# Two scatter-adds under way inside one expert, and the mark that frees an output slot moved behind GpSimd's split

## What is computed

```python
def block_fn(args):
    tok, w, e = args
    return swiglu(x_pad[tok], we_gate[e], we_up[e], we_down[e]) * w[:, None]

ys = lax.map(block_fn, (row_tok.reshape(n_blocks, MOE_BLOCK), row_w.reshape(n_blocks, MOE_BLOCK), block_e))
out = jnp.zeros((n_tok + 1, d), hf.dtype).at[row_tok].add(ys.reshape(n_rows, d))
```

## Time and profile before

| | us |
|---|---|
| median of 3 runs | 2760.79 (2759.81 to 2764.53) |
| the profiled execution's span | 2760.2 |
| TensorE busy in it | 2543.3 (92%) |
| GpSimd busy | 1397.6 (51%) |
| VectorE / ScalarE busy | 1569.3 / 1141.9 |

### The profile page before, as it was taken

The page is one execution under the profiler, slowest core; times in us unless marked ns, Lnnn a source line. Parts: engine busy times, 40 slices in busy tenths (PEclk is TensorE's granted clock), DMA queues, the critical chain, the costliest instruction groups (busy, mean ns, idle before and its releaser), DMA issues.

```text
span 2760.2 us, 49351 instructions
## 1 busy us (share of the span) xinstructions
PE 2543.3 (92%) x11232; PEld 1855.3 (67%) x11233; DVE 1569.3 (57%) x2796; ACT 1141.9 (41%) x1514; POOL 1397.6 (51%) x1726
## 2 busy tenths in 40 slices
PE   5999999998899997999999999999999999999980
PEld 2754665534466666777787877788877777787770
DVE  4689969986676775333343344435544554454535
ACT  5133222233233232344444444445555555555532
POOL 2011123024666664455555555566777677766751
PEclk9999999997899999999999999999999999999995
DMA  8262604465232325677777777788988898888978
GB/s 249 96 126 73 214 27 66 170 239 175 100 107 93 107 77 207 167 198 198 196 193 205 202 194 219 205 252 234 286 258 257 262 292 258 258 257 260 268 213 293
DMA packets 304953, 534.61 MB, mean 194 GB/s; under 512 B 38597, under 2 KB 204485, under 8 KB 304120
## 3 DMA queue, kind: packets, MB, share of 16 engines
q1 hardware_dynamic: 250248, 352.77, 38.7%
q0 software_dynamic: 51472, 173.70, 26.4%
q10 hardware_dynamic: 3168, 7.34, 0.7%
HBM read 395.75 MB, written 138.00 MB: 193 GB/s over the span
## 4 chain that ended last, share of the span: by engine, by line
PE 37%; issue 17%; POOL 9%; POOLq 7%; DVE 2%; DMA 1%; ACT 0%; SPq 0%; another core or an unknown queue 0%; ACTq 0%
PE psm L1168 27%; PE psm L1112 6%; POOL arena L2366 3%; PE psm L1161 2%; POOL arena L2363 2%; POOL st L2356 2%; POOLq L2362 2%; POOLq L2384 1%; POOLq L2383 1%; POOLq L2375 1%; POOL arena L2376 1%; PE psm L1190 1%; PE psm L1136 1%; POOL acc_d L2380 1%; POOL st L2388 1%
## 5 line engine op out<-in xcount | busy, mean ns | idle before, releaser
L1168 PE MATMUL psm<-whi,xhi 128*128 (+1 forms) x1424 | 574.3, 403 | 37.5 <-issue 24.6
L1168 PE MATMUL psm<-whi,xlo 128*128 (+1 forms) x1424 | 557.9, 392 | 0.0
L1168 PE MATMUL psm<-wlo,xhi 128*128 (+1 forms) x1424 | 556.9, 391 | 0.0
L2097 DVE TENSOR_TENSOR arena<-psm,arena 128x256 f32<-128x256 f32 x178 | 75.5, 424 | 603.3 <-ACT arena L1574 603.3
L1168 PEld LDWEIGHTS psm<-whi,xhi 128*128 128x128 f32 x1424 | 268.6, 189 | 109.6 <-issue 58.5
L2371 POOL TENSOR_TENSOR wlo<-raw,whi (+1 forms) x64 | 330.8, 5169 | 18.6 <-ACT whi L1606 18.6
L1168 PE MATMUL psm<-whi,hhi 128*128 (+1 forms) x712 | 295.5, 415 | 21.9 <-POOL wlo L2371 14.6
L1574 ACT ACTIVATE arena<-psm 128x256 f32<-128x256 f32 x178 | 68.5, 385 | 578.7 <-PE psm L1168 573.7
L2380 POOL DMA_INDIRECT acc_d<-arena x162 | 278.9, 1722 | 56.2 <-issue 51.1
L1168 PEld LDWEIGHTS psm<-whi,xlo 128*128 128x128 f32 x1424 | 268.2, 188 | 57.7
L1168 PEld LDWEIGHTS psm<-wlo,xhi 128*128 128x128 f32 x1424 | 269.1, 189 | 51.0
(11 more groups left out here) (387 smaller groups left out, 3996.3 us busy)
## 6 DMA issues: line engine op xcount, KB each, us to landing
raw<-in_we_gate_dram SPq DMA_DIRECT2D x64, 1024.0 KB
raw<-in_we_up_dram SPq DMA_DIRECT2D x64, 1024.0 KB
raw<-in_we_down_dram SPq DMA_DIRECT2D x64, 1024.0 KB, 5.1
arena<-in_w_ada_dram SPq DMA_DIRECT2D x12, 2048.0 KB
arena<-in_x_dram SPq DMA_DIRECT2D x32, 512.0 KB, 4.2
h_d<-arena SPq DMA_DIRECT2D x17, 512.0 KB, 2.7
arena<-in_w_in_dram SPq DMA_DIRECT2D x16, 512.0 KB, 5.4
mix_d<-bo SPq DMA_DIRECT2D x32, 256.0 KB, 2.3
```

Source lines behind the costliest of these rows:

```text
L1168: m = TE.matmul(o, a, w, start=(n == 0), stop=(n == len(todo) - 1))
L2097: tt(htmp, psm[:, bank, 0:DE], sigb, ALU.mult).then_inc(s_hm_ready, 1)
```

## The change

Scatter n no longer waits for the landing of scatter n - 1, unless its block begins an expert. To tell landings apart there are two semaphores, one for each slot (`s_ya_out0`, `s_ya_out1`), and two index columns. VectorE makes a row `fences` once, in `block_rows`: for each block the count that the *other* slot's semaphore must have reached before its scatter goes. It is 16 times the number of earlier blocks in that slot, one fewer of them where the block does not begin an expert, and at least 16; so inside an expert the wait asks only for the scatter three back. GpSimd fills the row `turns` from which it is made with an `iota` ahead of the routed stage. In the step, the wait for the scatter of block b - 2 and its mark now come last, behind the scatter and the split. Behind the loop, the last scatter still waits for its predecessor.

```diff
@@ block_rows (VectorE)
+                dve.wait_ge(s_turns_ready, 1)
+                do(V.tensor_copy(rone[:, 0:NB], turns))
+                do(stt(rone[:, 0:NB], news[:, 1:NB + 1], 16.0, rone[:, 0:NB], ALU.mult, ALU.add))
+                do(ts(fences, rone[:, 0:NB], 16.0, None, ALU.max))
                 V.tensor_copy(splits, bef).then_inc(s_br_ready, 1)
@@ GpSimd, before the table is read back
+            for o in (s_bo_out0, s_bo_out1):
+                pool.wait_ge(o, 16 * (len(bok) // 2))
+            PO.iota(turns, pattern=[[16, NB // 2], [0, 2]], base=0, channel_multiplier=0).then_inc(s_turns_ready, 1)
@@ add_block
-            def add_block(b, w):
+            def add_block(b, w, first=False):
                 c = pool.value_load(berow[0:1, bass.ds(b + (3 * P - NT), 1)], min_val=0, max_val=NCOL - 2)
-                PO.tensor_copy(idxs, tabl[:, bass.ds(c, 1), 0].bitcast(U32)).then_inc(s_idy_ready, 1)
+                PO.tensor_copy(idxs[w], tabl[:, bass.ds(c, 1), 0].bitcast(U32)).then_inc(s_idy_ready, 1)
+                if not first:
+                    x = pool.value_load(fences[0:1, bass.ds(b - (NT + 1), 1)], min_val=16, max_val=16 * NB)
+                    pool.wait_ge([s_ya_out0, s_ya_out1][1 - w], x)
                 pool.wait_ge(s_idy_ready, b - (NT - 1))
                 pool.wait_ge(s_y_act, b + 1)
                 hold()
-                PO.indirect_dma_start(acc_d, bass.IndirectOffsetOnAxis(idxs, 0), yb[w], None, compute_op=ALU.add).then_inc(s_ya_out, 16)
+                PO.indirect_dma_start(acc_d, bass.IndirectOffsetOnAxis(idxs[w], 0), yb[w], None, compute_op=ALU.add)\
+                  .then_inc([s_ya_out0, s_ya_out1][w], 16)
@@ step
                 gather(b + 3, b - (NT - 4), 1 - w)
-                if not first:
-                    pool.wait_ge(s_ya_out, (b - (NT + 1)) * 16)
-                    PO.tensor_tensor(st[:, 59:60], mhalf[:, :], mhalf[:, :], ALU.add).then_inc(s_y_free, 1)
-                add_block(b - 1, 1 - w)
+                add_block(b - 1, 1 - w, first)
                 with pool.If(f > 0):
                     split_low((o & 1) * WSLOT, o + 1)
+                if not first:
+                    pool.wait_ge([s_ya_out0, s_ya_out1][w], ((b - (NT + 2)) >> 1) * 16 + 16)
+                    PO.tensor_tensor(st[:, 54 + w:55 + w], mhalf[:, :], mhalf[:, :], ALU.add).then_inc(s_y_free, 1)
@@ behind the loop
-            before = pool.value_load(nbm[0:1, 0:1], min_val=TOPK - 1, max_val=NB)
-            pool.wait_ge(s_ya_out, before * 16)
+            pool.wait_ge(s_ya_out0, nb * 8)
             PO.tensor_tensor(st[:, 59:60], mhalf[:, :], mhalf[:, :], ALU.add).then_inc(s_y_free, 1)
-            add_block(nb + (NT - 1), 1)
-            pool.wait_ge(s_ya_out, nb * 16)
+            add_block(nb + (NT - 1), 1, first=True)
+            pool.wait_ge(s_ya_out1, nb * 8)
```

More of the change, by code:

```diff
@@ L363, in build @@
         s_idy_ready = sem("idy_ready")
-        s_ya_out = sem("ya_out")
+        s_ya_out0 = sem("ya_out0")
+        s_ya_out1 = sem("ya_out1")
+        s_turns_ready = sem("turns_ready")
         UNITS = [(g, k) for g in range(2) for k in range(KD)]
@@ L532, in build @@
         nbm = cut2(1, dt=I32, base=W)
-        idxs = cut2(1, dt=U32, base=W)
+        idxs = [cut2(1, dt=U32, base=W) for _ in range(2)]
         bef, news, rone = (cut2(NROW, base=W)[0:1, :] for _ in range(3))
@@ L545, in build @@
         ordi, splits = (ytok[0:1, n * NROW:(n + 1) * NROW].bitcast(I32) for n in range(2))
+        turns, fences = (bof[0:1, 5 * P + n * (NROW - 2):5 * P + (n + 1) * (NROW - 2)].bitcast(I32) for n in range(2))
         xg = [xbr[:, 0:1024], xbr[:, 1024:2048]]
```

## The result

The changed kernel takes 2723.6 us (median of 4 runs, 2719.33 to 2727.93) where the kernel before took 2762.66 beside it (4 runs, 2759.81 to 2766.76): a ratio of 0.9861, 95% interval 0.9837 to 0.9885. The forecast was 2724. The profiled execution spans 2717.6 us against 2760.2.

What follows compares the result with a forecast made beforehand. TensorE, nearly always busy in the routed stage, was taken as the bound, with gains only from its idle time there and from the end. Terms summed to 36.6 us less than 2760.79: forecast 2724 us, 8-in-10 range 2704 to 2764.

Steps and rivals of the forecast that it cites:

- 1, the wait for GpSimd's split: Before `down`: TensorE's wait for GpSimd's split goes, as scatters inside an expert no longer wait; -14.6 us.
- 3, the large stall: Where GpSimd's split meets VectorE's: half of 6.6 us of idle and low clock goes; -3.3 us, bounds +5 and -6.6.
- part 2: TensorE's wait for gathered rows goes, as gathers come earlier with the scatters; -4.3 us, bounds 0 and -4.3.
- part 4: TensorE's 24.6 us of "issue" idle before `gate_up` shrinks as scatter traffic moves earlier; -10 us, bounds +10 and -20.
- 5, the end: End of the routed stage: scatter 160 goes unserialized, so the last scatter follows earlier; -4.4 us, bounds 0 and -4.5.
- 6, what is added: GpSimd's added register load and second wait per scatter, 0.6 us, are covered by its spare time; cost 0.
- 7, the mark moved: GpSimd's mark comes up to 7 us later; ScalarE waits 0 to 1.5 us, TensorE is covered; cost 0, at most +15.
- The rule on one DMA: The skill's estimate of 3.2 us per scatter would leave no landing wait to remove; given no chance.
- A: Rival: only the wait itself moves, and new fence waits or slower transfers take the rest; 2749 us, chance 0.17.
- D: Rival: nearly all of TensorE's idle time goes, all terms at their lower bounds; 2711 us, chance 0.15.
- B: Rival: GpSimd's and VectorE's splits collide late in the stage if GpSimd's runs over 2.3 us later; 2785 us, chance 0.14.
- C: Rival: the late mark reaches TensorE, 31 pairs of splits at about 1 us each; 2755 us, chance 0.07.

Runs made afterwards that it cites:

- e9: Changed kernel with one of TensorE's register loads put ahead of the hidden-row transposes and the other dropped, in every second block: 2721.41 us, 0.9853 of the kernel before.
- e3: Changed kernel with the landing wait and the mark put back ahead of GpSimd's split, scatters still overlapping: 2739.84 us, 0.9922 of the kernel before.
- e2: Changed kernel with every scatter waiting for the landing of the one before, mark still behind the split: 2794.24 us, 1.0123 of the kernel before.
- e4: Changed kernel with the scatter replaced by a tiny counting instruction, routed rows never added: 2700.48 us, 0.9776 of the kernel before.
- e8: Changed kernel with scatters that write their rows instead of adding them: 2712.29 us, 0.9829 of the kernel before.
- e10: Changed kernel with four TensorE register loads ahead of `gate_up` in place of two: 2900.95 us, 1.0507 of the kernel before.
- e12: Changed kernel with TensorE's hidden-row transposes issued behind the loop's branch and register loads, at the next step's start: 2681.4 us, 0.9726 of the kernel before.
- e7: Changed kernel with its added register load done three times ahead of each scatter: 2745.63 us, 0.9937 of the kernel before.
- e5: Changed kernel with GpSimd's split, and the mark behind it, held until TensorE has done the next block's `gate_up`: 2735.3 us, 0.9909 of the kernel before.
- e11: Changed kernel with GpSimd's split held until the next block's products are wholly done, but mark and landing wait ahead of it: 2764.8 us, 1.0003 of the kernel before.
- e6: Changed kernel with GpSimd's split, and the mark behind it, held until the next block's `down` is done: 2879.87 us, 1.0431 of the kernel before.

## Why the prediction was right, point by point

**Bound.** TensorE as the bound, with a gain only from its idle time in the stage and from the end, held: the terms measured for the stage add up to 14.6 + 4.3 + 3.2 + 8.0 = 30.1 us of listed waits, and with the 3.4 us of clock at the stall it is 33.5 of the 33.6 found.

The list counts only from the end of the instruction before, though. Measured as in e9, against a start that overlaps the transposes by 0.24 us, the same 33.6 us divide differently: `down` lost 21.5 us before the change and 0.2 after it (parts 1 and 3), the transposes of gathered rows 5.0 and 0.1 (part 2), `gate_up` 50.2 and 46.5 (part 4), and 3.7 are left for the clock. So part 4 gave 3.7 us where the sum has 10, and parts 1 to 3 gave some 29 or 30 where it has 22.2. The mechanisms of parts 1, 2, 3 and 5 were right. That the forecast of 2724 us came within a microsecond is in part luck: these two errors cancel, and the medians taken side by side differ by 39.1 us where the sum has 36.6.

**1, the wait for GpSimd's split, -14.6.** Measured -14.6 in the list. The reason holds as well: the scatters of the changed kernel follow the copies by 2.3 us, e3, in which the mark stands where it stood, has none of this wait left, and with the fence always closed (e2) the time is above that of before.

**2, gathered rows, -4.3.** Measured -4.3, in the trace; no run takes it apart from the rest.

**3, the large stall, -3.3.** It went whole, 3.2 us of wait and the low clock (6.6 us), so the term was half of what it should have been. The margin of 0.5 us that I read from the earlier trace rows was about 1 us in the changed kernel's trace (2562.58 to 2563.63).

**4, "issue", -10.** Listed, it fell by 8.0 (24.6 to 16.6), in the bounds and near the value, but above the 10 to 15 us that I named as the sign of being right; with lost overlap counted it is 3.7, about a third of the term. The coincidence read from two rows was a real one: the table by microseconds shows it in five kernels, e4 and e8 tie it to the scatter's traffic. Both directions came true: between 1200 and 1880 us all such gaps fell from 20.7 us to 9.5, in the dense stretch they grew from 1.0 to 7.0, which I had listed as a sign of being wrong. What I did not see is what the gap is made of. "Waited for nothing that the profile shows" was TensorE's own register loads and branch, in sight in the code of `routed_step` and in the trace (under e10), and worth some 40 us (e12), about as much as the whole change. The change moved the loads that are stretched but did not make them fewer: 34 of 320 take over 0.4 us in either kernel.

**5, the end, -4.4.** Measured -4.4. The last scatter starts 2.5 us after the last copy, not 1.5 to 1.8.

**6, what is added, 0.** The weak step. "GpSimd has it" is true of its time (no split came late), but not of the scatter's start: in e7, two more loads moved the scatters by 0.7 us and cost 10.5 us in the traces, with TensorE's own loads stretched by 16.6 us more. By the same measure the one load of the change costs some microseconds that the sum has at 0; it wasn't run alone, so the figure is open. GpSimd's cover was the wrong question. The right one was what starts later behind the load, and what that meets.

**7, the mark moved, 0.** ScalarE waited longer for it than I estimated (122.9 us, 52 times, up to 3.2 us; I had 0 to 1.5 each), and no wait of TensorE's carries its name. I called the move free; e3 shows that, with scatters that overlap, it gains 16 us, because the wait for the landing moved with it and no longer holds back the split. The text counted every instruction that came ahead of the mark and forgot what came out from ahead of the split.

**The rule on one DMA.** The Trainium skill, "DMA: Bandwidth & Descriptors", "Anatomy of one DMA", gave an estimate of 3.2 us for a scatter. Measured were 8.2 us on average over 162 scatters, 5.9 without the add: the measurement decides, and the wait that it would have denied was there.

**The rivals.** A and D did not occur. B needed the split to be more than 2.3 us later: e5, 2.5 us late, overlapped by 2.0 us and cost nearly nothing, e3, with overlaps to 4.2 us, 1.6 us a meeting, e11 2.7. The threshold was well placed, the price (3.2 us and 3.4 of clock) two to four times too high. It is e11 that comes closest to it, at no gain over before. C's cause exists: 115 us of e6, with waits of up to 7.0 us for the mark, but its path runs over the transposes of hidden rows to `gate_up` and not over `h_low` to `down`. The changed kernel, at 3.2 us, stays below the point from which it counts.

## What to carry over

When a step is moved behind another, list also what it no longer holds back: a wait that travels with a mark can be worth more than the mark. An engine that has time to spare still sets when its transfers start, so an edit on it is to be costed by what those transfers meet.

Idle time marked "issue" on the engine that bounds the kernel can be explained: look in the code for register loads and branches at that place, ask the trace for their lines, and put them behind work that keeps the queue full, ahead of something that has to wait anyway. Doubling the suspected instructions (e10) prices them in a single run.

## What the runs showed of the hardware

- A register load on TensorE's queue with nothing to cover it costs 0.55 us on average (e10). Two of them and a loop's branch, with two transposes ahead, lose between nothing and 1.7 us beyond the transposes, by when the last scatter-add was started: most at 4 us after it, little from 7 us on.
- The load alone takes 0.30 us, and up to 1.6 us when it starts 2 to 5 us after a scatter-add's start (kernel before); without scatters never over 0.32 (e4).
- A scatter-add of 128 rows of 4 KB lands after 8.2 us on average (up to 11.2) in the changed kernel, where two can be under way, 5.9 us if it writes without adding.
- GpSimd's split of 4.6 us beside one of VectorE's: VectorE's piece takes 3.08 us at an overlap of 2.0 us (e5) and 5.64 at 4.6 (e11), instead of 1.22. It hardly advances while the other runs.
